# A decode step of a convolution layer and a sparse attention layer: products by kind, row transfers on another queue, sampled rows' projection as one operand

## What is computed

```python
def conformer_layer(x, conv_prev, g_pre, w_in, conv_w, conv_b, ln_g, ln_b, w_out, g_post):
    h = rms_norm(x, g_pre)
    a, b, z = jnp.split(h @ w_in, 3, axis=-1)
    glu = a * jax.nn.sigmoid(b)
    full = jnp.concatenate([conv_prev, glu], axis=1)
    c = depthwise_conv(full, conv_w) + conv_b
    y = jax.nn.silu(layer_norm(c, ln_g, ln_b)) * jax.nn.silu(z)
    return x + rms_norm(y @ w_out, g_post), full[:, -(CONV_W - 1):]

cmp, slc, win = kv_rows(x, kv_norm, w_kv)        # one key/value projection, three branches
kc, vc = compress(past and new cmp rows)         # small network over 32-row blocks
o = [attend(q, kc, vc), attend(q, selected slc blocks), attend(q, win rows)]
x + rms_norm(sum(gate * o * silu(z)) @ w_out, g_post)
```

## Time and profile before

| what | us |
|---|---|
| median of 3 runs | 876.22 (875.26 to 877.77) |
| the profiled execution | 875.5 |
| its span | 873.7 |
| PE busy | 849.5 (97%), 6246 matmuls |
| PEld busy | 761.8 |
| DVE busy | 546.9 (63%) |
| ACT busy | 479.9 (55%) |
| POOL busy | 308.3 (35%) |

### The profile page before, as it was taken

The page is one execution under the profiler, slowest core; times in us unless marked ns, Lnnn a source line. Parts: engine busy times, 40 slices in busy tenths (PEclk is TensorE's granted clock), DMA queues, the critical chain, the costliest instruction groups (busy, mean ns, idle before and its releaser), DMA issues.

```text
span 873.7 us, 16552 instructions
## 1 busy us (share of the span) xinstructions
PE 849.5 (97%) x6246; PEld 761.8 (87%) x6246; DVE 546.9 (63%) x1179; ACT 479.9 (55%) x940; POOL 308.3 (35%) x311
## 2 busy tenths in 40 slices
PE   7999999999999999999988999999999999999996
PEld 6999999955887778889978999999999999987774
DVE  6579999998967683333255555655565645536674
ACT  6667776633742543334376666767667676524241
POOL 2399888879050000003022333334343433300000
PEclk9999999999999999999999999999999999999999
DMA  9465433127259465067321323232323322472621
GB/s 250 116 176 152 119 101 80 58 49 240 67 166 377 178 214 164 10 157 209 82 57 25 74 52 89 56 73 50 73 50 74 73 50 50 93 236 86 207 87 37
DMA packets 158164, 99.51 MB, mean 114 GB/s; under 512 B 97202, under 2 KB 147026, under 8 KB 158005
## 3 DMA queue, kind: packets, MB, share of 16 engines
q1 hardware_dynamic: 143278, 79.30, 33.8%
q0 software_dynamic: 4896, 10.32, 3.4%
q10 hardware_dynamic: 9911, 8.84, 3.1%
HBM read 89.58 MB, written 18.85 MB: 124 GB/s over the span
## 4 chain that ended last, share of the span: by engine, by line
PE 91%; DVE 4%; ACT 3%; issue 1%; ACTq 1%; POOL 0%; DVEq 0%
PE psum L2377 7%; PE psum L2378 7%; PE psum L2379 7%; PE psum L2494 6%; PE psum L2003 6%; PE psum L2005 6%; PE psum L2004 6%; PE psum L2090 5%; PE psum L2203 4%; PE psum L2454 4%; PE psum L2204 4%; PE psum L2205 4%; PE psum L2424 4%; PE psum L2410 3%; PE psum L1984 2%; PE psum L2566 2%
## 5 line engine op out<-in xcount | busy, mean ns | idle before, releaser
L842 ACT ACTIVATE arena<-psum 128x512 f32<-128x512 f32 (+7 forms) x211 | 92.1, 473 | 145.3 <-PE psum L2379 66.4
L2377 PE MATMUL psum<-u_hi,tile_hi 128*128 128x288 f32 x464 | 140.5, 303 | 0.0
L2378 PE MATMUL psum<-u_lo,tile_hi 128*128 128x288 f32 x464 | 137.6, 297 | 0.0
L823 POOL TENSOR_SCALAR arena<-arena,kept 128x512 f32<-128x512 f32 (+3 forms) x128 | 90.2, 725 | 134.1 <-DVE kept L1806 134.1
L2379 PE MATMUL psum<-u_hi,tile_lo 128*128 128x288 f32 x464 | 136.7, 295 | 0.0
L1468 DVE SCALAR_TENSOR_TENSOR psum<-arena,psum 128x512 f32<-128x512 f32 x168 | 127.0, 756 | 6.0
L2003 PE MATMUL psum<-h_hi,tile_hi 128*128 128x288 f32 x352 | 104.3, 296 | 0.0
L2004 PE MATMUL psum<-h_lo,tile_hi 128*128 128x288 f32 x352 | 103.8, 295 | 0.0
L2005 PE MATMUL psum<-h_hi,tile_lo 128*128 128x288 f32 x352 | 103.8, 295 | 0.0
L2377 PEld LDWEIGHTS psum<-u_hi,tile_hi 128*128 128x128 f32 x464 | 87.4, 188 | 3.0 <-issue 2.6
L2378 PEld LDWEIGHTS psum<-u_lo,tile_hi 128*128 128x128 f32 x464 | 87.4, 188 | 0.3
(11 more groups left out here) (332 smaller groups left out, 1889.9 us busy)
## 6 DMA issues: line engine op xcount, KB each, us to landing
tile_whole<-in_b_w_in SPq DMA_DIRECT2D x64, 256.0 KB
tile_whole<-in_a_w_in SPq DMA_DIRECT2D x24, 512.0 KB
arena<-in_cmp_w SPq DMA_DIRECT2D x4, 2048.0 KB, 9.7
kvw_whole<-in_w_kv SPq DMA_DIRECT2D x6, 1024.0 KB, 14.7
bias_copies<-bias_line POOLq DMA_DIRECT2D x4, 1280.0 KB, 23.5
arena<-in_x_prompt SPq DMA_DIRECT2D x8, 512.0 KB, 6.4
kvw_whole<-in_a_w_out SPq DMA_DIRECT2D x4, 1024.0 KB, 11.4
arena<-bias_copies SPq DMA_DIRECT2D x16, 256.0 KB, 3.8
```

The source lines that it names most:

```text
L823: pool.tensor_scalar(L, L, rden[:, 8 + j:9 + j], gR[:, i, h:h + 1], ALU.mult, ALU.mult).then_inc(S["pn_ready"], 1)
L842: return nc.scalar.activation(out, in_, ACT.Copy, scale=scale)
L2377: pe.matmul(pb(b, HT), w_hi, u_hi[:, k, here], start=(k == 0), stop=False)
L2378: pe.matmul(pb(b, HT), w_hi, u_lo[:, k, here], start=False, stop=False)
```

## The change

- Start: `first_half` becomes `first_third`, which runs all eight blocks of one kind of product (high x high, then low weights, then low rows), so the waits for low parts come between kinds. Two groups of fillers go; the low weights of tile 1 move from DVE to POOL; DVE and ACT get another order there.
- The matmul of squares in `compress` comes after block 10 instead of 6; the transposes of new rows come before the second product of the compression, in another bank.
- The eight transfers of new convolution rows move from ACT's program to POOL's, behind the bias copies and the state copies. The state copies signal `page_in` instead of `late`; DVE, ahead of its first L1597, waits for the eight on `late`.
- The sampled rows of the first output projection (t=4) are one operand `y_pair` of high and low parts, in 32 matmuls; ACT copies the lower half of the result, DVE adds it to the upper. Two weight copies of ACT and halves of the low parts on DVE move ahead for it, and `turn_b(4)` moves from unit 2 to unit 3 of the key/value projection.
- Attention steps: ACT loads the exponential's table between the two first gate copies; denominators and scaling of the compressed branch in the first step come behind the first units; in every second step `y_product(m, 0)` comes before the next low half.
- End: `vnew` and `pts` have 128 partitions, zeroed by POOL, so that the third part of the value product contracts 128 rows too; SP issues the first four new rows early; a part of the last projection moves into the loop; the two sums of the sampled rows come apart; their last projection goes to two banks, each squared and multiplied by the gain as it is done.

The diff, cut:

```diff
...
+        y_pair = over("y_pair", R_G + 8320, KD, 2 * NS)
+        out_part = at(R_G + 3072, D, p1=NS)
...
-        pts = at(R_G + 8192, 2, 3, P)
-        vnew = at(R_G + 8960, 6, CH, p1=DS)
+        pts = at(R_X + 6 * CH, 2, 3, P)
+        vnew = at(R_X, 6, CH)
...
+sp.wait_ge(S["zeroes"], ZEROED["rest"])
+for n in range(4):
+    new_v_rows(n)
...
+pool.wait_ge(S["hi_ready"], 2)
+pool.tensor_tensor(out=tile_lo[:, 1], in0=tile_w[:, 1], in1=tile_hi[:, 1], op=ALU.subtract).then_inc(S["w1_lo"], 1)
...
+pool.wait_ge(S["page_in"], 16)
...
-pool.dma_start(O["conv_sample"][0, :, 0:W - 1 - DS, :], I["state_conv"][0, :, DS:W - 1, :]).then_inc(S["late"], 16)
-pool.dma_start(O["win_sample"][:, 0:PAST], I["state_win"]).then_inc(S["late"], 16)
+pool.dma_start(O["conv_sample"][0, :, 0:W - 1 - DS, :], I["state_conv"][0, :, DS:W - 1, :]).then_inc(S["page_in"], 16)
+pool.dma_start(O["win_sample"][:, 0:PAST], I["state_win"]).then_inc(S["page_in"], 16)
+pool.wait_ge(S["co_ready"], 2)
+for b in range(DB):
+    pool.dma_start(O["conv_sample"][0, b, W - 1 - DS:W - 1], conv_out_s[DS * b:DS * b + DS]).then_inc(S["late"], 16)
...
+        if n == 0 and j == 2:
+            probs_cmp(0)
...
+pool.wait_ge(S["tile_mm"], tile_done(N_TILES - 1))
+pool.wait_ge(S["t_done"], turned_cmp(KD - 1))
+pool.memset(vnew, 0.0).then_inc(S["zeroes"], 1)
+pool.memset(pts, 0.0).then_inc(S["zeroes"], 1)
...
-first_hi(3)
+act.wait_ge(S["early_mm"], 1)
+copy(line[:, 0:SEQ], pb(0, SEQ, p1=H), -1.0).then_inc(S["line_part"], 1)
+act.wait_ge(S["early_mm"], 2)
+copy(pe_sb, pb(1, 2, 16)).then_inc(S["line_part"], 1)
...
+first_hi(3)
 first_hi(4)
-act.wait_ge(S["early_mm"], 1)
-copy(line[:, 0:SEQ], pb(0, SEQ, p1=H), -1.0).then_inc(S["line_part"], 1)
-act.wait_ge(S["early_mm"], 2)
-copy(pe_sb, pb(1, 2, 16)).then_inc(S["line_part"], 1)
...
-copy(conv_out_s[0:NS], pb(6, D, p1=NS)).then_inc(S["co_ready"], 1)
-act.wait_ge(S["co_ready"], 2)
-for b in range(DB):
-    act.dma_start(O["conv_sample"][0, b, W - 1 - DS:W - 1], conv_out_s[DS * b:DS * b + DS]).then_inc(S["co_out"], 16)
+copy(conv_out_s[0:NS], pb(2, D, p1=NS)).then_inc(S["co_ready"], 1)
...
+    src = pb(2 * (t % 2), D, p1=r)
+    if t == TT - 1:
+        copy(out_part, pb(0, D, p0=NS, p1=2 * NS)).then_inc(S["part_out"], 1)
+        act.wait_ge(S["centred"], KD + 2)
+        src = out_part
+    nc.scalar.activation(junk_b[0:r], src, ACT.Square, accum_out=ss[0:r, 0:1]).then_inc(S["sq_b"], 1)
...
+    if t == 3:
+        kv_weight_hi(0)
...
+    if t == 3:
+        kv_weight_hi(1)
...
-        copy(y_hi[:, :, SEQ:NT], y_whole[:, :, SEQ:NT]).then_inc(S["hh_ready"], 1)
-    if t == 3:
-        for c in range(2):
-            kv_weight_hi(c)
+        act.wait_ge(S["co_ready"], 2)
+        copy(y_pair[:, :, 0:NS], y_whole[:, :, SEQ:NT]).then_inc(S["hh_ready"], 1)
...
-for n in range(2):
-    z_copy(n, 2 + 4 * n)
+z_copy(0, 2)
+nc.scalar.activation(sd[:, 6:7], ident[:, 0:1], ACT.Exp)
+z_copy(1, 6)
...
-act.wait_ge(S["fo_mm"], TT)
 act.wait_ge(S["sq_a"], TT + 4)
-nc.scalar.activation(junk_c[:, 0:D // 2], pb(4, D // 2), ACT.Square, accum_out=ss[:, 4:5]).then_inc(S["sq_a"], 1)
+for c in range(2):
+    act.wait_ge(S["fo_mm"], TT + c)
+    nc.scalar.activation(junk_c[:, c * CH:(c + 1) * CH], pb(4 + c, CH), ACT.Square,
+                         accum_out=ss[:, 4 + c:5 + c]).then_inc(S["sq_a"], 1)
...
+first_mean(4)
 first_lo(2)
-first_mean(4)
...
+first_turn(5)
 first_lo(3)
-first_weight_lo(1)
 dve.wait_ge(S["hh_ready"], 5)
 V.tensor_tensor(out=h_lo[:, :, 3 * P:4 * P], in0=h_whole[:, :, 3 * P:4 * P], in1=h_hi[:, :, 3 * P:4 * P],
                 op=ALU.subtract).then_inc(S["lo_pool"], 1)
-first_turn(5)
...
-    V.tensor_tensor(out=y_lo[:, :, here], in0=y_whole[:, :, here], in1=y_hi[:, :, here], op=ALU.subtract).then_inc(S["hl_ready"], 1)
+    hi, lo = (y_hi[:, :, here], y_lo[:, :, here]) if t < TT - 1 else (y_pair[:, :, 0:NS], y_pair[:, :, NS:2 * NS])
+    V.tensor_tensor(out=lo, in0=y_whole[:, :, here], in1=hi, op=ALU.subtract).then_inc(S["hl_ready"], 1)
...
+        summed = pb(2 * (t % 2), D, p1=r)
+        if t == TT - 1:
+            dve.wait_ge(S["part_out"], 1)
+            V.tensor_tensor(out=out_part, in0=summed, in1=out_part, op=ALU.add).then_inc(S["centred"], 1)
+            summed = out_part
         dve.wait_ge(S["sq_b"], t + 1)
         mean_sq(0, r, "ms_bc")
         dve.wait_ge(S["sd_bc"], 2 * t + 1)
         link(dve, V.reciprocal(rs[0:r, 0:1], sd[0:r, 0:1]))
-        V.scalar_tensor_tensor(out=scaled_b[0:r], in0=pb(2 * (t % 2), D, p1=r), scalar=rs[0:r, 0:1],
+        V.scalar_tensor_tensor(out=scaled_b[0:r], in0=summed, scalar=rs[0:r, 0:1],
...
-            dve.wait_ge(S["co_out"], 16 * (1 + DB))
+            dve.wait_ge(S["co_out"], 16)
+            dve.wait_ge(S["late"], 16 * DB)
...
+        if t == 3:
+            for c in range(2):
+                kv_weight_lo(c, slice(0, KD // 2))
...
-            for ks in (slice(0, KD // 2), slice(KD // 2, KD)):
-                for c in range(2):
-                    kv_weight_lo(c, ks)
+            for c in range(2):
+                kv_weight_lo(c, slice(KD // 2, KD))
...
-den_of_cmp(0)
 for n in range(N_STEPS):
     m, br = n // 2, 1 + n % 2
     sums(n)
     den_of(n, 0)
+    if n == 0:
+        den_of_cmp(0)
...
-    next_lo(tile_over(n, 1))
     if br == 1:
         y_product(m, 0)
-    elif m + 1 < KD:
+    next_lo(tile_over(n, 1))
+    if br == 2 and m + 1 < KD:
...
+def y_sample_sum(br):
+    ys = yT[:, :, SEQ:NT]
+    dve.wait_ge(S["ys_mul"], 2 * (3 * DB - 1 + br))
+    if br:
+        dve.wait_ge(S["y_s"], 1)
+    V.tensor_tensor(out=ys, in0=ys, in1=y_br[:, br], op=ALU.add).then_inc(S["y_s"], 1)
...
+    if w == 2 * DB + 2:
+        y_sample_sum(0)
+y_sample_sum(1)
...
+dve.wait_ge(fy_out[0], 16 * 2)
+for c in range(2):
+    dve.wait_ge(S["sq_a"], 2 * TT + c)
+    n_dve[0] += 1
+    V.tensor_tensor(out=y_out[:, 0, c * CH:(c + 1) * CH], in0=pb(4 + c, CH), in1=gpost_s[:, c * CH:(c + 1) * CH],
+                    op=ALU.mult).then_inc(dve_step, 1)
+dve.wait_ge(S["fo_mm"], TT + 2)
+V.tensor_scalar(ms[:, 4:5], pb(3, 1), 1.0 / D, EPS, ALU.mult, ALU.add).then_inc(S["ms_a"], 1)
...
+V.scalar_tensor_tensor(out=y_out[:, 0, 0:D // 2], in0=y_out[:, 0, 0:D // 2], scalar=rs[:, 4:5],
+                       in1=x1_back[:, 0, 0:D // 2], op0=ALU.mult, op1=ALU.add).then_inc(S["fy"], 1)
...
-for t in range(1, 3):
-    turn_a(t)
-    keep_busy(4)
+turn_a(1)
+keep_busy(4)
+turn_a(2)
 small_tables()
 turn_a(3)
-keep_busy(4)
...
-        if squares and j == 6:
+        if squares and j == 10:
...
+def first_third(c, hf, part):
+    w, h = ((tile_hi, h_hi), (tile_hi, h_lo), (tile_lo, h_hi))[part]
+    last = 1 if hf or c == 0 else 2
     for k in range(KD):
-        out, here = pb((2, 0)[c] + hf, HT), slice(hf * HT, hf * HT + HT)
-        pe.matmul(out, tile_hi[:, c, k], h_hi[:, k, here], start=(k == 0), stop=False)
-        pe.matmul(out, tile_hi[:, c, k], h_lo[:, k, here], start=False, stop=False)
-        ins = pe.matmul(out, tile_lo[:, c, k], h_hi[:, k, here], start=False, stop=(k == KD - 1))
+        ins = pe.matmul(pb((2, 0)[c] + hf, HT), w[:, c, k], h[:, k, hf * HT:hf * HT + HT],
+                        start=(part == 0 and k == 0), stop=(part == last and k == KD - 1))
...
+pe.wait_ge(S["hh_ready"], 3)
+pe.wait_ge(S["hi_ready"], 1)
+first_third(0, 0, 0)
+pe.wait_ge(S["lo_pool"], 1)
+first_third(0, 0, 2)
 pe.wait_ge(S["hl_ready"], 3)
-pe.wait_ge(S["lo_pool"], 1)
-first_half(0, 0)
+first_third(0, 0, 1)
+pe.wait_ge(S["line_part"], 3)
+pe.wait_ge(S["hi_ready"], 2)
+first_third(1, 0, 0)
 turn_a(4)
-pe.wait_ge(S["line_part"], 3)
-pe.wait_ge(S["lo_pool"], 2)
-first_half(1, 0)
-pe.wait_ge(S["hl_ready"], 5)
-pe.wait_ge(S["lo_pool"], 3)
+first_third(1, 0, 1)
+pe.wait_ge(S["w1_lo"], 1)
+first_third(1, 0, 2)
+pe.wait_ge(S["hh_ready"], 6)
...
-            ins = first_half(c, 1)
+            first_third(c, 1, 0)
+            first_third(c, 1, 2)
+            pe.wait_ge(S["hl_ready"], 5)
+            ins = first_third(c, 1, 1)
...
+pe.wait_ge(S["new_packed"], DB)
+for k in range(KD):
+    ins = pe.transpose(pb(2, KD, P, p1=NS)[:, k], new_rows[:, k], ident)
+ins.then_inc(S["co_tr"], 1)
 pe.wait_ge(S["hid_ready"], 4)
 pe.wait_ge(S["z_ready"], KD)
 for b in range(DB):
     ins = product(pb(4, DB, P, p1=60)[:, b], ((hid[:, ht, 60 * b:60 * b + 60], w2_sb[:, 1, ht]) for ht in range(2)))
 ins.then_inc(S["cs_mm"], 1)
-pe.wait_ge(S["new_packed"], DB)
-for k in range(KD):
-    ins = pe.transpose(pb(6, KD, P, p1=NS)[:, k], new_rows[:, k], ident)
-ins.then_inc(S["co_tr"], 1)
...
-        split_out(t, 1).then_inc(S["o_mm"], 1)
-        split_out(t, 0).then_inc(S["o_mm"], 1)
+        pe.wait_ge(S["hl_ready"], 10)
+        pe.wait_ge(S["lo_ready"], 4)
+        for p in (1, 0):
+            stacked(p, y_pair, (ow_hi(p), kvw_rest[:, 2 * p:2 * p + 2])).then_inc(S["o_mm"], 1)
...
-    if n == 2:
+    if n == 3:
...
+pe.wait_ge(S["zeroes"], ZEROED["rest"])
...
-for h in halves_at[0]:
```

(46 more changed lines are left out.)

25 lines of the change are left out of this document (8 added, 17 removed).

## The result

The changed kernel takes 885.8 us (median of 4 runs, 885.54 to 885.94) beside 876.5 of the kernel before (also 4 runs): ratio 1.0106, 95% interval 1.0088 to 1.0123. It is 9.3 us slower, where 5.3 had been forecast. Its profiled execution takes 885.54, with a span of 883.7.

The account below looks back on a forecast made before the run. TensorE matmuls were taken as the bound (91% of the span). Stall shift 14.1, first step -5.6, tail -4.7 and clock +1.7 gave +5.5: 881.0 against 875.5, put at 881.5 as a median, range 863 to 889 us.

Parts of the forecast that it names:

- R, the last landing: Landing of the last of eight row transfers on POOL's queue: about 298 us, bounds 293 and 303.
- From R to the stacked product: From DVE's first write into the rows' region to the key/value projection's first stacked product: 54.5 us, as before.
- Sampled rows' projection: First output projection, sampled rows: PE saves 3.75 us, later waits offset it; net 0, bounds -1.9 (gain) and +1.9.
- Start: First half tile's products by kind, two filler groups gone: 1.9 us gained, bounds 0.8 and 2.4.
- Compress and transposes: Compress stage, matmul of squares later and new-row transposes earlier: 1.7 us gained, bounds 0 and 2.4.
- Row transfers off ACT: At the t=1 projection, PE's 1.13 us wait for low weights goes: 1.1 us gained.
- First step: First attention step, PE's waits for POOL and DVE almost go: 5.6 us gained, bounds 2.5 and 7.
- Tail: Sampled attention to last projection, 128-row form and shorter waits: 4.7 us gained, bounds 1.5 and 6.
- The fourth rival: Attention step and tail gains fail, with the stall: 889 us; no separate chance given.
- The rule weighed in the prediction: POOL's DMA queue works in order, completing once all 16 engines post: last row lands at 298, by the opposite 262.
- One sign that the prediction took for it: POOL's earlier copies landed after 23.5, 29.6 and 46.2 us in issue order, although the second was smaller.
- the first rival: Row transfers on POOL land early, at 262 to 279, without a stall: median 861.2 us, range 857 to 867; chance 0.22.

Follow-up runs that it names:

- before_moved: The kernel before with only the eight row transfers moved behind POOL's bias and state copies, state copies on their own semaphore: 894.13 us, ratio 1.0206.
- the three orders: The changed kernel with the eight row transfers ahead of, between or (unedited) behind POOL's copies: 864.23, 866.37 and 885.8 us.
- rf_step_old: `rows_first` with the attention steps back in the order of the kernel before: 869.76 us, ratio 0.9927.
- rows_first: The changed kernel with POOL issuing the eight row transfers ahead of the bias and state copies: 864.23 us, ratio 0.9869.

## Why the prediction was right, and where its terms were off

The direction, the mechanism and the place were right: PE idles before the second transposes for 18.3 us (13 to 17 forecast), DVE waits 21.0 (19), the rows end just behind the window state, and the gains before that are lost in the stall. The chance of 0.22 for rows that land early is refuted by `before_moved` and by the three orders; the size was short by 4.5 of 10.0, and one term carries it; in the others a slip and two omissions cancelled by luck.

- **R, the last landing**: 298 forecast, 302.4 measured, inside its bounds of 293 and 303. Two steps are in it. POOL was to issue 2 earlier "with the gains above"; it issued 1.2 later (249.61 against 248.39), since the start had lost 1.2 instead of gaining 1.9, and the gains of the compress stage lie on PE, not on the path that releases POOL. And the eight rows were given 0.4 behind the window state; they took 1.8 to 2.0.
- **From R to the stacked product**: 54.5, and 1.7 added for the clock, 56.2 together; measured 56.1, and that is luck. In the trace before, 6.4 of the 54.5 lie between DVE's write and PE's second transposes, because PE was still at the t=1 projection. Behind a stall nothing is left to do there: 3.8 us (302.42 to 306.20), and the prediction itself had 3.6 just ahead of the 54.5. With its own 3.6 the stretch is 51.7 and the forecast +2.7 instead of +5.5. The 2.8 too many stood in for what was missing: the clock cost 2.1 to 2.4 behind the stall (1.7 forecast), and the projection's net 0 was a loss of 1.8 (inside its bound of 1.9).
- **Sampled rows' projection**: of the 3.75 saved on PE, 3.0 are left behind a wait of 0.5 (8.2 from the first of the 32 matmuls to the next transposes, 11.2 before). In the changed kernel the first unit of the key/value projection starts 0.5 earlier against the second transposes (26.6 behind them, 2.1 of it clock, against 25.0 before), the lower end of 0.4 to 2.3, and the third waits 2.4, in the middle of 1.3 to 3.2. Net 0 took the upper half of the one and the middle of the other. Without the stall the loss is 2.1 (50.2 against 48.1), with or without a fall of the clock.
- **Start**: 1.9 gained forecast, 1.2 lost, outside the bounds of 0.8 and 2.4. The fillers were priced by their own length, and what they hold up was left out. DVE's new order was not followed to POOL, which works beside it. Where the clock stayed, the stage gained 0.4.
- **Compress and transposes**: 1.7 forecast; the stretch up to them gained 2.5, just above the upper bound of 2.4. **Row transfers off ACT**: 1.1 forecast, 1.2.
- **First step**: 5.6 forecast; 5.0 by the landmarks, 5.1 to 5.5 by undoing it. **Tail**: 4.7 forecast, 5.1 measured; the 128-row form alone 2.3 forecast, 2.4 to 2.6.

By landmarks, 4.4 (R) - 0.1 + 0.6 (step) - 0.4 (tail) make the 4.5 that the sum was short of; the -0.1 is the lucky term. The fourth rival's 889 is also off by its own terms: 881.7 + 5.6 + 4.7 is 892.

The rule weighed in the prediction (the Trainium skill, "DMA: Bandwidth & Descriptors", "Queues, rings and completion order") came out as the traces have it: the last landings in front, in the middle and at the end of one queue were 2.5, 26.4 and 43.5 us after issue, and a semaphore of its own for the copies changed nothing about them. The page says it of the queues of SP and ACT; here POOL's shows it. One sign that the prediction took for it was weaker than it looked: the two state copies of before share a semaphore, so the order of their landings, 29.6 and 46.2, is the order of issue by the way they are counted. The same page's section "Why a DMA increments its semaphore by 16 and not by 1" says that all 16 engines post for a POOL transfer. The trace agrees: eight transfers have 128 steps, and these come in two halves, 64 by 285.3 and 64 behind the window state's last packets, as they would if half of the engines had that copy to move and the others did not. The window state's own 16 steps come alike, 8 by 283.6 and 8 from 297.2 to 300.4. So the first rival was half right with "half the queue's engines may be done with the large copies early": half were early, and all eight rows still waited for the others. The steps do not name their engines, so this reading of the halves is an inference from counts.

## What to carry to other kernels

A semaphore of its own frees a wait from what it counts, not from what stands ahead in the queue: before a transfer is moved, read the landing times of the bulk copies already issued there, and put what somebody waits for in front. Where several transfers share a semaphore, only the landing of the last is sure. A saving of matmuls is worth what the next engine in the chain leaves of it. A fall of the clock behind a wait costs only what no later wait would have cost anyway: behind the 2.4 us wait of the key/value projection it cost nothing at the stretch's end; in the attention steps it came on top (420.9 us from the first stacked product to the attention of the sampled rows in `rf_step_old`, 414.2 in `rows_first`, while PE's waits there differ by 4.0). Filler matmuls are priced with the clock of the stretch behind them, over several executions, since the same start had it both ways.

## What was not expected of the hardware

- A DVE subtraction of 128x512, neither operand of it a matmul result, took 2.87 us beside a POOL subtraction of the same kind, 0.69 without one; it ended 0.55 behind POOL's end (29.65 against 29.10). POOL's own went from 2.40 to 2.54. Other DVE work beside such a POOL subtraction, reading the matmul results instead, was not stretched: 0.94 for 128x768 at 18.80, while POOL ran 18.73 to 21.1.
- Small transfers of POOL's queue, 32 KB from on-chip memory, landed 2.0 us after issue in the median when they were first in it, faster than the 5.2 of the 8 KB ones in the earlier trace rows.
- The start without the fillers was granted the full clock in five executions and half of it for some 3 us in four.
- Eight transfers whose data packets had run by 284.3 gave the last of their signals at 302.2: half of the 128 came with the data, half behind a 4 MB copy that stood ahead of them in POOL's queue.
